# LayerNorm channel sums folded on GpSimd, and three convolution taps a slot in the last two chunks, in a Conformer and stick-breaking attention layer

## The chip, the cores and the metric

One core of a Trainium2 chip runs the whole program: TensorE (matmul), VectorE, ScalarE, GpSimd, and SyncE, which here issues every DMA. In the profile they are PE (and PEld for its weight loads), DVE, ACT, POOL and SP. The metric is the device time of one execution in microseconds (us); lower is better.

## The reference, cut to what matters

```python
h = _rmsnorm(x, g_mix)
a, gate, q, k, v = jnp.split(h @ w_in, [...], axis=-1)
u = a * jax.nn.sigmoid(gate)                                   # 512 channels
c = _causal_dwconv(u_ext, w_dw) + b_dw                         # 31 taps, each channel by itself
c = jax.nn.silu(_layernorm(c, g_cn, b_cn)) @ w_pw              # LayerNorm over the 512 channels
o = _stick_breaking(rmsnorm(q), rmsnorm(k_all), v_all, ...)    # 8 heads x 64
x = x + jnp.concatenate([c, o], axis=-1) @ w_out
f = jax.nn.relu(_rmsnorm(x, g_ff) @ w_ff1)
x = x + (f * f) @ w_ff2                                        # 4096 hidden
```

It is computed for a prompt of 2048 frames and for 64 further frames of a running stream (the sample), in fp32. `_layernorm` takes the mean over the channels, subtracts it, squares, takes the mean of the squares and scales. Weight matmuls are made of three passes over values split in a high and a low part.

## The kernel before, in words

The prompt is cut into four chunks of 512 frames (0 to 3); the 64 sample frames ride with chunk 3. Channels lie on the 128 partitions, so the convolution's sum of a chunk is four blocks (k = 0 to 3) of 128x512, held in `cacc` (in `cacc_second` for chunk 1). In chunk 3 a tap covers 606 columns, and the LayerNorm runs once over 512 columns and once over the sample's 64.

The order of all work is written out by hand in slots. A slot is one step of TensorE's main work, and every engine walks the same list of slots, each in its own program order. Chunk c+1's tail of convolution, LayerNorm, pointwise projection (`pw`) and attention is woven into the slots of the feed-forward of chunk c (`window(c)`: eight rounds e of 16 slots, of which the first eight are `f1` slots, 12 matmuls each, and the last eight are `f2` slots, 12 matmuls each). For chunk 0 the tail is woven into `front()`: 92 slots of six matmuls that compute the projections of chunk 1. `window(2)`, `window(1)` and `window(0)` thus hold the tails of chunks 3, 2 and 1.

Within a slot an engine takes its parts in a fixed order. VectorE first splits new weights if due (`w_s<-w_raw`), then runs `convolve(late_taps)`, then the step of `ln`, then `pw`, then its add of a finished `f2` result (`resid<-ps`) or, in every second `f1` slot, the low part of the hidden values (`hid_lo`), which waits for three passes of ScalarE over the matmul result. TensorE does the step of `ln`, then `pw`, then the slot's main matmuls, then the steps of attention.

The last `LATE[c]` taps of a chunk (20, 43, 36, 28 of 124) run in the slots before `ln0(c)`, two a slot. Then LN_STEPS steps follow, one a slot: 0 TensorE multiplies each of the four blocks with a 128x128 matrix of ones (`ones`, true fp32), which adds up the channels over blocks and partitions into PSUM; 1 VectorE takes off the mean (L1803), ScalarE squares into `csq` (L1402); 2 TensorE does the same four matmuls over `csq`; 3 and 4 the reciprocal root; then the scaling, the sigmoid, GpSimd's `cid` (L1162) and the split into `cT_hi` and `cT_lo`. The sample's piece follows eight slots behind. `pw_slot(c)` is the slot after the last step, `att_first(c)` is five slots later (nine for chunk 0), and attention fills the slots to `att_past(c)` (58 for chunk 0, 116 otherwise) evenly.

| chunk | ln0 before / after | pw_slot before / after | att_first before / after |
|---|---|---|---|
| 0 | 10 / 10 | 22 / 24 | 31 / 33 |
| 1 | 22 / 22 | 34 / 36 | 39 / 41 |
| 2 | 18 / 12 | 30 / 26 | 35 / 31 |
| 3 | 14 / 10 | 34 / 32 | 39 / 37 |

Weights pass through a ring of eight slabs of 1 MB (`w_s`, RING = 8). `weight_order()` puts the two `pw` slabs behind the four `f1` slabs of round `e == pw_slot(c + 1) // 16`. The load of slab n may go out when slab n - 8 is free (L774), and an `f2` slab is free when all the `f2` slots of its round are done. SyncE issues in program order, so what stands behind a DMA that waits, waits too.

## Time and profile before

| | |
|---|---|
| median of 3 runs | 2778.92 us (2776.28 to 2780.08) |
| span of the profiled execution, from its first to its last instruction | 2777.2 us |
| mean granted TensorE clock of the core | 0.990 |
| PE busy, DVE busy, ACT busy, POOL busy | 97%, 60%, 39%, 16% |
| HBM traffic over the span | 221 GB/s |

The span is 1.7 us under the median of the runs. A matmul of 128x512 in a run of them takes 0.39 us from its start to its end in the rows, but the next starts 0.23 us after it: they overlap, and it is the distance between starts that counts. A true fp32 matmul stands in the rows as two MATMUL records. "PEclk" is the granted clock as a share of 2.4 GHz; 0.5 is 1.2 GHz. The time in square brackets is how long the engine was idle before the row, and who ended that.

### The profile page before, as it was taken

How to read it: one execution, taken by the hardware profiler on the slowest of the kernel's cores; microseconds unless marked ns; L12 is line 12 of the kernel's file. 1: busy time of each engine (PE TensorE's matmuls, PEld its weight loads, DVE VectorE, ACT ScalarE, POOL GpSimd, SP SyncE). 2: the span in 40 equal slices, each digit the busy share in tenths (PEclk: the TensorE clock that was granted, in tenths of full speed). 3: DMA queues.
4: the chain of work that ended last, by engine and by line, in shares of the span. 5: the costliest groups of instructions: out<-in, count | busy, mean ns of one | idle time of the engine just before them, and what ended most of it. 6: DMA issues, size and time to landing. Idle time of an engine off the chain costs nothing. (4 is left out here: it accounts for less than half of the span.)

```text
span 2777.2 us, 37645 instructions
## 1 busy us (share of the span) xinstructions
PE 2687.2 (97%) x14000; PEld 2270.3 (82%) x14000; DVE 1663.9 (60%) x2621; ACT 1069.5 (39%) x2146; POOL 453.3 (16%) x462
## 2 busy tenths in 40 slices
PE   8988899999999999999999999999999999999999
PEld 6757778788887887788888797778888887998998
DVE  6996767577763576377775368627888842222122
ACT  4434524455552122355553212335666631221211
POOL 2122210022210010032221102103333310000000
PEclk9999999999999999999999999999999999999999
DMA  9795797697769568455554747845355456443532
GB/s 330 255 349 188 237 355 266 259 336 253 256 218 375 214 233 282 184 209 185 168 187 165 284 186 237 291 163 190 118 181 191 150 188 248 187 177 122 212 152 95
DMA packets 262048, 616.21 MB, mean 222 GB/s; under 512 B 23217, under 2 KB 159409, under 8 KB 213741
## 3 DMA queue, kind: packets, MB, share of 16 engines
q1 hardware_dynamic: 261869, 613.80, 61.8%
q8 instruction: 115, 1.88, 0.3%
q14 instruction: 64, 0.52, 0.1%
HBM read 444.79 MB, written 168.94 MB: 221 GB/s over the span
## 5 line engine op out<-in xcount | busy, mean ns | idle before, releaser
L2020 PE MATMUL ps<-h2T_hi,w_s 128*128 128x512 f32 (+2 forms) x1312 | 469.2, 358 | 7.9 <-DMA w_s<-w_scratch 3.9
L2022 PE MATMUL ps<-h2T_hi,w_s 128*128 128x512 f32 (+2 forms) x1312 | 458.3, 349 | 0.0
L1174 POOL TENSOR_TENSOR beta<-beta,stay 128x512 f32<-128x512 f32 (+3 forms) x328 | 313.0, 955 | 889.5 <-DVE stay L1859 853.4
L2021 PE MATMUL ps<-h2T_lo,w_s 128*128 128x512 f32 (+2 forms) x1312 | 457.9, 349 | 0.0
L1929 DVE TENSOR_TENSOR resid<-ps,resid 128x512 f32<-128x512 f32 x256 | 174.6, 687 | 261.3 <-PE ps L2285 260.6
L1451 ACT ACTIVATE stay<-ps 128x512 f32<-128x512 f32 (+3 forms) x328 | 174.8, 533 | 347.2 <-PE ps L2221 227.1
L2283 PE MATMUL ps<-w_s,hid_hi 128*128 128x512 f32 x768 | 308.3, 401 | 0.0
L2284 PE MATMUL ps<-w_s,hid_lo 128*128 128x512 f32 x768 | 299.9, 390 | 0.0
L2285 PE MATMUL ps<-w_s,hid_hi 128*128 128x512 f32 x768 | 299.8, 390 | 0.0
L1526 ACT ACTIVATE ps<-ps 128x512 f32<-128x512 f32 (+1 forms) x160 | 81.3, 508 | 542.7 <-PE ps L2022 542.7
L2020 PEld LDWEIGHTS ps<-h2T_hi,w_s 128*128 128x128 f32 x1312 | 248.0, 189 | 38.3 <-DMA w_s<-w_scratch 4.0
L1859 DVE TENSOR_TENSOR_SCAN stay<-stay,stay,ones 128x512 f32<-128x512 f32 x192 | 274.4, 1430 | 0.0
L2022 PEld LDWEIGHTS ps<-h2T_hi,w_s 128*128 128x128 f32 x1312 | 247.8, 189 | 30.9
L2021 PEld LDWEIGHTS ps<-h2T_lo,w_s 128*128 128x128 f32 x1312 | 248.2, 189 | 26.6 <-issue 1.0
L1651 DVE SCALAR_TENSOR_TENSOR cacc<-uT,vecs,cacc 128x512 f32<-128x512 f32 (+1 forms) x360 | 259.6, 777 | 1.5
L1939 DVE TENSOR_TENSOR hid_lo<-ps,hid_hi 128x512 fp32r<-128x512 f32 x96 | 66.3, 691 | 261.8 <-ACT hid_hi L1536 261.8
L1869 DVE TENSOR_TENSOR aT_lo<-ps,aT_hi 128x512 fp32r<-128x512 f32 (+3 forms) x328 | 189.6, 578 | 14.6 <-ACT aT_hi L1463 8.8
L2221 PE MATMUL ps<-a_k,a_q 128*128 128x512 f32 (+3 forms) x640 | 186.9, 371 | 8.8 <-DMA a_k<-k_scratch 6.9
L2231 PE MATMUL ps<-ident,beta 128*128 128x128 f32 (+1 forms) x1104 | 175.1, 274 | 7.4 <-DVE aT_lo L1869 7.3
L1463 ACT CAST aT_hi<-ps 128x512 fp32r<-128x512 f32 (+3 forms) x328 | 173.6, 529 | 19.3 <-PE ps L2231 14.7
L1452 ACT ACTIVATE beta<-ps 128x512 f32<-128x512 f32 (+3 forms) x328 | 173.6, 529 | 0.0
L2285 PEld LDWEIGHTS ps<-w_s,hid_hi 128*128 128x128 f32 x768 | 144.2, 188 | 31.9
(217 smaller groups left out, 5179.1 us busy)
## 6 DMA issues: line engine op xcount, KB each, us to landing
w_s<-w_scratch SPq DMA_DIRECT2D x282, 1024.0 KB, 7.5
w_scratch<-w_s SPq DMA_DIRECT2D x94, 1024.0 KB, 8.3
w_raw<-in_w_ff SPq DMA_DIRECT2D x64, 512.0 KB, 5.7
a_k<-k_scratch SPq DMA_DIRECT2D x80, 256.0 KB, 3.8
a_v<-v_scratch SPq DMA_DIRECT2D x80, 256.0 KB, 4.0
a_q<-q_scratch SPq DMA_DIRECT2D x64, 256.0 KB, 4.4
w_raw<-in_w_in SPq DMA_DIRECT2D x20, 512.0 KB, 7.7
mix_scratch<-ohl SPq DMA_DIRECT2D x66, 128.0 KB, 3.0
```

Of the source, the lines that this page charges most:

```text
L1174: nc.gpsimd.tensor_tensor(v[0:q.r, 0:n], v[0:q.r, 0:n], stay_of(q.z)[0:q.r, 1:n + 1], ALU.mult).then_inc(s_a, 1)
L1651: nc.vector.scalar_tensor_tensor(out=acc, in0=uT[:, k, tap:tap + wd], scalar=vecs[:, k, tap:tap + 1], in1=acc, op0=ALU.mult, op1=ALU.add). ...
L1859: nc.vector.tensor_tensor_scan(v[0:q.r, 0:q.n][:, ::-1], v[0:q.r, 0:q.n][:, ::-1], ones[0:q.r, 0:1].to_broadcast([q.r, q.n]), init, ALU.mu ...
L1869: ins = nc.vector.tensor_tensor(aT_lo[:, o, 0:full, q.t * P:q.t * P + q.r], bank[:, 0:full * q.r].rearrange("p (a b) -> p a b", a=full), a ...
L2020: nc.tensor.matmul(out, w[0], x[0], start=start, stop=False)
L2021: nc.tensor.matmul(out, w[0], x[1], start=False, stop=False)
L2022: return nc.tensor.matmul(out, w[1], x[0], start=False, stop=stop)
L2221: ins = nc.tensor.matmul(ps[0:q.r, Z_BANK + q.z % 2, 0:q.n], x, a_k[:, k0:k0 + q.n], start=v == 0, stop=v == 1)
L2231: ins = nc.tensor.transpose(ps[0:w, T_BANK + q.z % 2, b * q.r:(b + 1) * q.r], beta[q.z % 4][0:q.r, b * P:b * P + w], ident[0:q.r, 0:q.r])
L2283: nc.tensor.matmul(o, hid_hi[x][:, k, q0:q0 + r], wh[:, c0:c0 + BANK], start=k == 0, stop=False)
L2284: nc.tensor.matmul(o, hid_lo[x][:, k, q0:q0 + r], wh[:, c0:c0 + BANK], start=False, stop=False)
L2285: ins = nc.tensor.matmul(o, hid_hi[x][:, k, q0:q0 + r], wl[:, c0:c0 + BANK], start=False, stop=k == 3)
```

## The change

Three things. First, GpSimd adds the four blocks (two adds into `csq`, then one more) before the mean, and the four squared blocks before the variance; TensorE then does one matmul with `ones` where it did four. Second, these adds have steps of their own: LN_STEPS is 14 instead of 12, and all later steps move by one or by two. Third, chunks 2 and 3 issue three late taps a slot, so `ln0` of chunk 2 goes from 18 to 12 and that of chunk 3 from 14 to 10.

```diff
-LN_STEPS = 12
+LN_STEPS = 14
+def taps_a_slot(c):
+    return 3 if c > 1 else 2
 def ln0(c):
-    return (LATE[c] + 1) // 2
+    return -(-LATE[c] // taps_a_slot(c))
...
         def late_taps(c, slot):
-            return range(min(TAPS, TAPS - LATE[c] + 2 * slot), min(TAPS, TAPS - LATE[c] + 2 * slot + 2))
+            n = taps_a_slot(c)
+            return range(min(TAPS, TAPS - LATE[c] + n * slot), min(TAPS, TAPS - LATE[c] + n * (slot + 1)))
...
 # GpSimd
             def ln(c, n, step):
                 a, q0, w = conv_pieces(c)[n]
                 lb = c + n
-                k = step - 5
+                if step == 0:
+                    if c == 1:
+                        pool.wait_ge(out_ps, 8)
+                    pool.wait_ge(kvq_ps, 12 * c + 3 * len(tiles(c)))
+                    if n:
+                        pool.wait_ge(yn_ok, CB * lb)
+                    for h in range(2):
+                        for k in (2 * h, 2 * h + 1):
+                            pool.wait_ge(taps, TAPS * c + taps_in_order[c].index((k, CW - 1)) + 1)
+                        nc.gpsimd.tensor_tensor(csq[:, h, 0:w], conv_sum(c, 2 * h, a, w), conv_sum(c, 2 * h + 1, a, w),
+                                                ALU.add).then_inc(folded, 1)
+                    pool.wait_ge(folded, 6 * lb + 2)
+                    nc.gpsimd.tensor_tensor(csq[:, 0, 0:w], csq[:, 0, 0:w], csq[:, 1, 0:w], ALU.add).then_inc(folded, 1)
+                if step == 3:
+                    for h in range(2):
+                        pool.wait_ge(sq_ok, CB * lb + 2 * h + 2)
+                        nc.gpsimd.tensor_tensor(csq[:, 2 * h, 0:w], csq[:, 2 * h, 0:w], csq[:, 2 * h + 1, 0:w],
+                                                ALU.add).then_inc(folded, 1)
+                    pool.wait_ge(folded, 6 * lb + 5)
+                    nc.gpsimd.tensor_tensor(csq[:, 0, 0:w], csq[:, 0, 0:w], csq[:, 2, 0:w], ALU.add).then_inc(folded, 1)
+                k = step - 7
...
 # ScalarE: squares at step 2 (was 1), Ln and Exp at 5 (was 3), sigmoids from 7 (was 5), high parts from 9 (was 7)
 # VectorE: mean taken off at step 2 (was 1), lnv at 5 (was 3), scaling from 6 (was 4), products from 8, low parts from 10
 # TensorE
             def ln(c, n, step):
                 a, q0, w = conv_pieces(c)[n]
                 lb = c + n
-                if step == 0:
+                if step == 1:
                     if n:
                         pe.wait_ge(xc_ok, CB * lb)
-                    for k in range(CB):
-                        pe.wait_ge(taps, TAPS * c + taps_in_order[c].index((k, CW - 1)) + 1)
-                        ins = nc.tensor.matmul(ps[:, Z_BANK, 0:w], ones[:], conv_sum(c, k, a, w), start=k == 0, stop=k == CB - 1)
-                    ins.then_inc(mean_ps, 1)
-                if step == 2:
+                    pe.wait_ge(folded, 6 * lb + 3)
+                    nc.tensor.matmul(ps[:, Z_BANK, 0:w], ones[:], csq[:, 0, 0:w], start=True, stop=True).then_inc(mean_ps, 1)
+                if step == 4:
                     if n:
                         pe.wait_ge(var_ok, lb)
-                    for k in range(CB):
-                        pe.wait_ge(sq_ok, CB * lb + k + 1)
-                        ins = nc.tensor.matmul(ps[:, Z_BANK + 1, 0:w], ones[:], csq[:, k, 0:w], start=k == 0, stop=k == CB - 1)
-                    ins.then_inc(var_ps, 1)
+                    pe.wait_ge(folded, 6 * lb + 6)
+                    nc.tensor.matmul(ps[:, Z_BANK + 1, 0:w], ones[:], csq[:, 0, 0:w], start=True, stop=True).then_inc(var_ps, 1)
```

Three places show how the instructions move. The first is VectorE in `window(0)`, at the LayerNorm of chunk 1 (slots 21 to 25), before: `hid_lo` is the low part of the hidden values, `w_s<-w_raw` the split of a new weight slab, and the rows that wait for `mean_ps` take off the mean.

```order
L1651 SCALAR_TENSOR_TENSOR cacc_second_72<-uT,vecs,cacc_second_72 128x512 [waits taps]
L1939 TENSOR_TENSOR hid_lo_103<-ps,hid_hi_102 128x512 [waits f_hi]
L1611 TENSOR_TENSOR w_s<-w_raw,w_s 128x1024 [waits hi_done]
L1803 SCALAR_TENSOR_TENSOR cacc_second_69<-ps,cacc_second_69 128x512 [waits mean_ps]
L1803 SCALAR_TENSOR_TENSOR cacc_second_70<-ps,cacc_second_70 128x512
```

The same place in the changed kernel:

```order
L1675 SCALAR_TENSOR_TENSOR cacc_second_72<-uT,vecs,cacc_second_72 128x512 [waits taps]
L1963 TENSOR_TENSOR hid_lo_103<-ps,hid_hi_102 128x512 [waits f_hi]
L1635 TENSOR_TENSOR w_s<-w_raw,w_s 128x1024 [waits hi_done]
L1963 TENSOR_TENSOR hid_lo_103<-ps,hid_hi_102 128x512 [waits f_hi]
L1635 TENSOR_TENSOR w_s<-w_raw,w_s 128x1024 [waits hi_done]
L1827 SCALAR_TENSOR_TENSOR cacc_second_69<-ps,cacc_second_69 128x512 [waits mean_ps]
L1827 SCALAR_TENSOR_TENSOR cacc_second_70<-ps,cacc_second_70 128x512
```

The subtraction of the mean now stands behind a second `hid_lo` (that of slot 23) and a second weight split. The second place is TensorE in `window(2)`, at the first `pw` of chunk 3, which waits for its slab (`w_in2`), before:

```order
L2021 MATMUL ps<-h2T_lo_84,w_s 128x512
L2022 MATMUL ps<-h2T_hi_83,w_s 128x512
L2020 MATMUL ps<-cT_hi,w_s 128x512 [waits w_in2,c_lo]
L2021 MATMUL ps<-cT_lo,w_s 128x512
L2022 MATMUL ps<-cT_hi,w_s 128x512
```

And in the changed kernel:

```order
L2304 MATMUL ps<-w_s,hid_lo_103 128x512
L2305 MATMUL ps<-w_s,hid_hi_102 128x512
L2044 MATMUL ps<-cT_hi,w_s 128x512 [waits w_in2,c_lo]
L2045 MATMUL ps<-cT_lo,w_s 128x512
L2046 MATMUL ps<-cT_hi,w_s 128x512
```

Before, the 24 matmuls of two `f1` slots (`h2T`) stood between the last `f2` matmul of round 1 (`hid_hi`) and this `pw`; now it follows that matmul at once. The third place is SyncE in `front()`, where attention of chunk 0 begins: `a_q` and `a_k` are loads of queries and keys, `w_s` of weight slabs. Before:

```order
L895 DMA a_q<-q_scratch 128x2x256 [waits z_ps]
L774 DMA w_s<-w_scratch 128x2048 [waits w_st2,pw_ps]
L774 DMA w_s<-w_scratch 128x2048 [waits w_st3,pw_ps]
L774 DMA w_s<-w_scratch 128x2048 [waits ag_ps] x2
L886 DMA a_k<-k_scratch 128x512 [waits z_ps]
```

And in the changed kernel:

```order
L901 DMA a_q<-q_scratch 128x2x256 [waits z_ps]
L780 DMA w_s<-w_scratch 128x2048 [waits w_st3,pw_ps]
L780 DMA w_s<-w_scratch 128x2048 [waits w_st4,pw_ps]
L780 DMA w_s<-w_scratch 128x2048 [waits ag_ps]
L892 DMA a_k<-k_scratch 128x512 [waits z_ps]
```

Three slabs instead of four are issued between the first query load and the next keys.

## Rows read from the trace of the kernel before

**Rows 1.** The page, part 1: busy time and share of each engine.
```profile
PE 2687.2 (97%) x14000; PEld 2270.3 (82%) x14000; DVE 1663.9 (60%) x2621; ACT 1069.5 (39%) x2146; POOL 453.3 (16%) x462
```
**Rows 2.** Timeline of PE, chunk 0's LayerNorm: start us, us, instruction, [idle before, releaser].
```profile
172.18 1.88 PE L2178 MATMUL ps<-cacc,ones 128*128 128x512 f32 x4
...
177.56 1.19 PE L2178 MATMUL ps<-cacc,ones 128*128 128x512 f32 x2 [1.90 <-DVE cacc L1651]
...
182.86 3.59 PE L2185 MATMUL ps<-csq,ones 128*128 128x512 f32 x8
...
186.52 0.39 PE L2021 MATMUL ps<-hT_second_lo,w_s 128*128 128x512 f32 x1
```
**Rows 3.** Timeline of PE, the sample's two sums in chunk 3.
```profile
1809.27 1.00 PE L2178 MATMUL ps<-cacc,ones 128*128 128x64 f32 x8
```
**Rows 4.** Timeline of PE, DVE and ACT at chunk 1's LayerNorm.
```profile
487.88 2.84 PE L2178 MATMUL ps<-cacc_second,ones 128*128 128x512 f32 x6 [1.59 <-DVE cacc_second L1651]
...
487.07 2.07 DVE L1651 SCALAR_TENSOR_TENSOR cacc_second<-uT,vecs,cacc_second 128x512 f32<-128x512 f32 x3
...
490.80 2.48 DVE L1803 SCALAR_TENSOR_TENSOR cacc_second<-ps,cacc_second 128x512 f32<-128x512 f32 x4
498.09 0.69 DVE L1939 TENSOR_TENSOR hid_lo<-ps,hid_hi 128x512 fp32r<-128x512 f32 x1 [4.81 <-ACT hid_hi L1536]
498.69 1.21 DVE L1611 TENSOR_TENSOR w_s<-w_raw,w_s 128x1024 fp32r<-128x1024 f32 x1
...
491.51 2.42 ACT L1402 ACTIVATE csq<-cacc_second 128x512 f32<-128x512 f32 x4 [3.29 <-DVE cacc_second L1803]
496.24 0.58 ACT L1526 ACTIVATE ps<-ps 128x512 f32<-128x512 f32 x1 [2.30 <-PE ps L2022]
```
**Rows 5.** The line of GpSimd's multiply of two tiles: duration ns min/median/max.
```profile
L1174 POOL TENSOR_TENSOR beta<-beta,stay x328: 408/1092/2011, 229.4 to 2259.1; 128x512 f32<-128x512 f32 x96, 128x127 f32<-128x127 f32 x32, 128x383 f32<-128x383 f32 x32, 64x191 f32<-64x191 f32 x4
```
**Rows 6.** Timeline of DVE, chunk 2's taps in window(1).
```profile
1072.72 2.73 DVE L1651 SCALAR_TENSOR_TENSOR cacc<-uT,vecs,cacc 128x512 f32<-128x512 f32 x4
...
1078.43 0.69 DVE L1929 TENSOR_TENSOR resid<-ps,resid 128x512 f32<-128x512 f32 x1 [0.46 <-PE ps L2285]
```
**Rows 7.** Timeline of DVE and ACT, chunk 3's taps in window(2).
```profile
1747.03 3.12 DVE L1651 SCALAR_TENSOR_TENSOR cacc<-uT,vecs,cacc 128x606 f32<-128x606 f32 x4
...
1763.49 0.58 ACT L1526 ACTIVATE ps<-ps 128x512 f32<-128x512 f32 x1 [3.63 <-PE ps L2022]
```
**Rows 8.** Timeline of PE, four waits elsewhere.
```profile
246.94 0.45 PE L2221 MATMUL ps<-a_k,a_q 128*128 128x128 f32 x1 [6.07 <-DMA a_k<-k_scratch]
...
1169.45 0.79 PE L2020 MATMUL ps<-h2T_hi,w_s 128*128 128x512 f32 x1 [3.88 <-DMA w_s<-w_scratch]
...
1845.89 0.47 PE L2020 MATMUL ps<-cT_hi,w_s 128*128 128x512 f32 x1 [0.56 <-DMA w_s<-w_scratch]
1861.65 0.80 PE L2020 MATMUL ps<-cT_hi,w_s 128*128 128x512 f32 x1 [3.23 <-DVE pwo L1839]
```
**Rows 9.** Windows: us, busy us (x) of PE, PEld, DVE, ACT, POOL; PEclk, DMA share, GB/s.
```profile
240.00:270.00 30.00, 22.92 (x125) 19.95 (x123) 21.29 (x37) 14.78 (x40) 8.15 (x11) 0.83 0.57 175
270.00:300.00 30.00, 25.57 (x161) 21.77 (x160) 28.65 (x51) 21.00 (x58) 14.99 (x15) 1.00 0.67 193
...
1150.00:1180.00 30.00, 25.61 (x102) 20.48 (x101) 4.29 (x8) 7.33 (x16) 1.05 (x2) 0.89 0.66 260
...
1780.00:1880.00 100.00, 95.92 (x436) 76.72 (x434) 30.47 (x65) 36.55 (x67) 5.83 (x8) 0.98 0.50 187
```
**Rows 10.** Timeline of SP (issues) and, last, of PE where round 2's first matmul starts.
```profile
230.86 2.46 SPq L774 DMA_DIRECT2D w_s<-w_scratch  x4
233.36 0.74 SPq L886 DMA_DIRECT2D a_k<-k_scratch  x1
...
1838.36 0.39 PE L2020 MATMUL ps<-h2T_hi,w_s 128*128 128x512 f32 x1
```
**Rows 11.** The line of the slab loads, 1838 to 1850: from issue to landing.
```profile
DMA to landing us min/median/max: 4.7/8.9/10.9
```

More of the change, by code:

```diff
@@ L492, in build @@
         vp_out = [sem(f"vp_out{i}") for i in range(2)]
-        lg_ok, sd_ok, id_ok, nwt = sem("lg_ok"), sem("sd_ok"), sem("id_ok"), sem("nwt")
-        mean_ps, xc_ok, sq_ok, var_ps, var_ok, lnr_ok, yn_ok, sg_ok, cm_ok, c_hi, c_lo, cvo_ps, cvo_ok, cvo_out = (
-            sem(n) for n in ("mean_ps", "xc_ok", "sq_ok", "var_ps", "var_ok", "lnr_ok", "yn_ok", "sg_ok", "cm_ok",
+        lg_ok, sd_ok, id_ok = sem("lg_ok"), sem("sd_ok"), sem("id_ok")
+        folded, mean_ps, xc_ok, sq_ok, var_ps, var_ok, lnr_ok, yn_ok, sg_ok, cm_ok, c_hi, c_lo, cvo_ps, cvo_ok, cvo_out = (
+            sem(n) for n in ("folded", "mean_ps", "xc_ok", "sq_ok", "var_ps", "var_ok", "lnr_ok", "yn_ok", "sg_ok", "cm_ok",
                              "c_hi", "c_lo", "cvo_ps", "cvo_ok", "cvo_out"))
@@ L1396, in ln @@
                 nt = len(tiles(c))
-                if step == 1:
-                    if n:
-                        act.wait_ge(yn_ok, CB * lb)
+                if step == 2:
                     for k in range(CB):
@@ L1402, in ln @@
                         nc.scalar.activation(csq[:, k, 0:w], conv_sum(c, k, a, w), ACT.Square).then_inc(sq_ok, 1)
-                if step == 3:
+                if step == 5:
                     act.wait_ge(var_ok, lb + 1)
@@ L1408, in ln @@
                     nc.scalar.activation(unused[:], ident[:, 0:1], ACT.Sigmoid)
-                k = step - 5
+                k = step - 7
                 if 0 <= k < CB:
@@ L1415, in ln @@
                                          bias=vecs[:, k, CW + 2:CW + 3], scale=vecs[:, k, CW + 1:CW + 2]).then_inc(sg_ok, 1)
-                if step == 7 and n == 0:
+                if step == 9 and n == 0:
                     for m in (2 * nt - 2, 2 * nt - 1):
@@ L1422, in ln @@
                     act.wait_ge(vo_out[1], 16 * (2 * c + 2))
-                k = step - 7
+                k = step - 9
                 if 0 <= k < CB:
@@ L1799, in ln @@
                 lb = c + n
-                if step == 1:
+                if step == 2:
                     dve.wait_ge(mean_ps, lb + 1)
@@ L1804, in ln @@
                                                        in1=conv_sum(c, k, a, w), op0=ALU.mult, op1=ALU.add).then_inc(xc_ok, 1)
-                if step == 3:
+                if step == 5:
                     dve.wait_ge(var_ps, lb + 1)
                     nc.vector.tensor_scalar(lnv[:, 0:w], ps[:, Z_BANK + 1, 0:w], 1.0 / CC, EPS, ALU.mult, ALU.add).then_inc(var_ok, 1)
-                if step == 4:
+                if step == 6:
                     dve.wait_ge(sd_ok, lb + 1)
                     nc.vector.scalar_tensor_tensor(out=ntmp[:, 0:w], in0=lnr[:, 0:w], scalar=-0.5, in1=lnr[:, 0:w],
-                                                   op0=ALU.mult, op1=ALU.mult).then_inc(nwt, 1)
-                    dve.wait_ge(nwt, 2 * lb + 1)
-                    nc.vector.tensor_tensor(ntmp[:, 0:w], ntmp[:, 0:w], lnv[:, 0:w], ALU.mult).then_inc(nwt, 1)
-                    dve.wait_ge(nwt, 2 * lb + 2)
+                                                   op0=ALU.mult, op1=ALU.mult).then_inc(lnr_ok, 1)
+                    dve.wait_ge(lnr_ok, 3 * lb + 1)
+                    nc.vector.tensor_tensor(ntmp[:, 0:w], ntmp[:, 0:w], lnv[:, 0:w], ALU.mult).then_inc(lnr_ok, 1)
+                    dve.wait_ge(lnr_ok, 3 * lb + 2)
                     nc.vector.scalar_tensor_tensor(out=lnr[:, 0:w], in0=ntmp[:, 0:w], scalar=1.5, in1=lnr[:, 0:w],
                                                    op0=ALU.add, op1=ALU.mult).then_inc(lnr_ok, 1)
-                    dve.wait_ge(lnr_ok, lb + 1)
+                    dve.wait_ge(lnr_ok, 3 * lb + 3)
                     dve.wait_ge(xc_ok, CB * (lb + 1))
-                for k in {4: (0,), 5: (1, 2), 6: (3,)}.get(step, ()):
+                for k in {6: (0,), 7: (1, 2), 8: (3,)}.get(step, ()):
                     nc.vector.tensor_tensor(conv_sum(c, k, a, w), conv_sum(c, k, a, w), lnr[:, 0:w],
                                             ALU.mult).then_inc(yn_ok, 1)
-                k = step - 6
+                k = step - 8
                 if 0 <= k < CB:
@@ L1827, in ln @@
                                             ALU.mult).then_inc(cm_ok, 1)
-                k = step - 8
+                k = step - 10
                 if 0 <= k < CB:
```

## The prediction

> **What bounds the kernel now.** I read the page first: PE is busy for 97% of the span and no other engine for more than 60% [rows 1]. So the time is TensorE's list of slots, and only three things change it: the length of its work, its waits, and stretches at a lower clock. Next came the groups of instructions and the timeline of PE at the LayerNorms, for the price of the matmuls that go; then DVE and ACT at the same places, because TensorE will now wait for a chain through them and GpSimd; then the list of PE's waits over the whole span, because nearly every step of the three tails moves by two to six slots, and waits that hang on a slot number move too.
>
> The price of a matmul with `ones`: four of them start at 182.86, and the second ordinary matmul behind them starts at 186.52 [rows 2]. Less the 0.23 of one ordinary matmul that is 3.43 us, 0.86 each. For the sample's 64 columns eight records take 1.00 us, so 0.25 for each of four [rows 3].
>
> **Part 1: matmuls removed.** Each full piece loses six of eight: 4 pieces x 6 x 0.86 = 20.6 us. The sample loses 6 x 0.25 = 1.5. Together -22.1 us, all of it on the path.
>
> **Part 2: the waits for the folds.** A fold of 128x512 isn't in the trace; the nearest row is GpSimd's multiply of two tiles, 1.09 us in the median, 2.01 at most [rows 5]. I take 1.1 us, since it is the same instruction with another operation. The bounds are 0.8 (three quarters of the median) and 2.0. Only two folds lie behind the last tap: that of blocks 2 and 3 and the final one, 2.2 us. Before the variance it is again two, behind the last square. TensorE covers the first with one slot of work (step 0), the second with what is left of three.
>
> Chunk 0, where a slot is six matmuls, 1.37 us. The last tap ends at 177.5 (TensorE's last fourth waits for it until 177.56), while TensorE is at slot 10 at 172.18 and its next ordinary matmul starts at 178.12 [rows 2]: 5.9 us for 3.4 of work, so 2.4 us of waits. Now slot 11 begins at 173.55 and the mean can start at 177.5 + 2.2 + 0.2 for semaphores = 179.9: a wait of 6.3 us, +3.9. Mean taken off and squares need some 3.3 us after it, the folds 2.2: that is 186.4, and TensorE is then at about 187, so no second wait.
>
> Chunk 1, slots of 12 matmuls, 2.72 us. The last three taps run 487.07 to 489.1, and TensorE waits 1.59 us to 487.88 [rows 4]. TensorE comes to slot 23 at 485.26 + 2.72 = 488.0, the folds end at 491.4: wait 3.5 instead of 1.6, +1.9. The variance is worse. The order of instructions shows the subtraction of the mean behind the `hid_lo` of slot 23 and a weight split. Slot 23 ends at 495.0; three ScalarE passes (496.24 to the 498.09 of the next row) are 1.85, `hid_lo` 0.6, the split 1.2, the four subtractions 2.5, the last square 0.7 behind them [rows 4], the folds 2.2: 504.1. TensorE is at slot 26 at 500.5. +3.6 us.
>
> Chunk 2: four taps take 2.73 with overlap, 0.66 each [rows 6]. From 1072.72 the six taps of slots 8 and 9, two adds, three taps, an add and three taps end at 1082.5; slot 10's result comes at 1078.4, so slot 13 begins at 1083.9 and the folds end at 1084.8: +0.9. The variance comes out +0.5 by the same count (subtraction behind slot 13's add). Chunk 3: a tap of 606 columns takes 0.76, and from 1747.03 DVE has four times six taps and a `hid_lo`, and four more taps: 1770.75. TensorE begins slot 8 at 1763.4 [rows 7], slot 11 at 1771.6, the folds end at 1773.0: +1.4, +0.3 for a `hid_lo` that is late at slot 9, +0.5 at the variance. The sample's mean in slot 19 now waits for the scaling of the main piece at slot 18 and three short folds: +1.7 (0 to 3.4).
>
> Sum of waits: 3.9 + 1.9 + 3.6 + 1.4 + 2.2 + 1.7 = +14.7 us.
>
> **Part 3: the clock.** After a wait of 3.23 us ending at 1861.65 the granted clock over 1780 to 1880 is 0.98, and after 3.88 us it is 0.89 over 30 us, after 6.07 us 0.83 over 30 us [rows 8, 9]: 1.7 to 2 us, 3.3 and 5.1 us lost, some of it within the wait. For chunk 1's two waits of 3.5 us I take 1.7 each, for chunk 0 0.9 more than now (it has such a stretch already). +4.3. The lower bound is 0, if no clock falls.
>
> **Part 4: slabs and keys.** Chunk 3's `pw` moves from slot 34 to slot 32, the first of round 2, and its slab may be loaded only when the `f2` slots of round 1 are done: at that very moment (second place of the order). TensorE was there at 1838.36 [rows 10]; the first of the loads lands 4.7 us after its issue [rows 11], at 1843.3; the second slab was waited for until 1845.89 at slot 34, by 0.56 us [rows 8]. Now the first `pw` waits 5.0 us and, 1.4 us of matmuls later, again until 7.5 us after the slot's start: 6.2 of waits, against 0.6. With a clock stretch between those of 3.88 and 6.07 us this is +5.6 + 2.6 = **+8.2 us**. Nothing covers it: `pw` stands ahead of the slot's own matmuls.
>
> Chunk 2's wait of 3.88 us at 1169.45 goes. It is for slab `f1` of round 2, third quarter, which takes the place of `pw`'s first slab: free in slot 34, needed in slot 36, with SyncE held by the `pw` stores. Now it is free at slot 30. With its clock (3.3 us less 0.4 within the wait) -6.8. A wait of 0.6 for `pw`'s slab in chunk 1 goes as well (slot 34 to 36).
>
> In `front()` the keys of the third head are issued at 233.36 behind four slabs, and TensorE waits 6.07 us for them [rows 8, 10]. Now three slabs stand ahead. Between 233 and 246.9 some 4 MB moved, so a slab is worth about 3 us: -2.9, the clock unchanged.
>
> Sum: +8.2 - 6.8 - 0.6 - 2.9 = -2.1.
>
> **Part 5: attention.** Chunk 0's 41 steps now fill 25 slots, not 27. In 270 to 300 DVE is busy for 28.65 of 30 us [rows 9], so packing more steps there costs up to two slots of TensorE's work, 2.7 us, and nothing if TensorE is the later; I take +1.3. Chunks 2 and 3 get four and two slots more, chunk 1 two fewer; PE isn't idle there by more than tenths, 0.
>
> **The sum:** -22.1 + 14.7 + 4.3 - 2.1 + 1.3 = **-3.9 us**: a span of 2773.3 us, and with the 1.7 us that the median lies above the span 2775.0.
>
> **Where the skill and the rows differ.** The median of 1.09 us was measured while DVE scanned beside it, and the longest of that line is 2.01 [rows 5]. The Trainium skill, GPSIMD Engine Reference, "Specifications", says that GpSimd shares its SBUF interfaces with VectorE, with contention when a VectorE instruction has two SBUF inputs. The taps are such instructions; by that rule the folds would run nearer to the 2.0 us, and the rival below on slow folds is what it would make of the time. "Engine selection" on the same page says to add on VectorE, as GpSimd is some 2x slower; 0.69 us on DVE against 1.09 here agrees in direction.
>
> **The rivals.** About 0.2%, 5.6 us, is what this measurement can tell from no change.
>
> Forecast, 44%: the gain of the matmuls is nearly eaten, result within 0.2%, 2773.4 to 2784.
>
> First rival, 38%, faster by more than 0.2%: the waits are half of what I count, because VectorE's lag at the end of the taps shrinks once TensorE is the one that is later, or the clock doesn't fall after 3.5 us. Half of 19.0 is 9.5: 2765.5. For it: the wait of 1.59 us was followed by no slower matmuls. Against it: chunk 1's chain is counted from rows with no slack in it. If all waits vanished the time would be 2756; I give that 3% of these 38.
>
> Second rival, 10%, slower: the folds take 2.0 us. Two folds behind the last tap and two behind the last square in four pieces are 16 folds x 0.9 = +14.4: 2789.4. It decides from a fold of about 1.7 us on. It would also lengthen the taps beside them. Against it: GpSimd stands still otherwise in these slots, and after the last tap DVE has little to do.
>
> Third rival, 8%, slower: `front()` is bound by DVE and not by TensorE. Chunk 0's terms above are -5.2 for matmuls, +3.9 and +0.9 for the wait and its clock, -2.9 for the keys, +1.3 for attention: -2.0. If DVE sets the pace, matmuls and keys give nothing back, DVE stands still while GpSimd folds (+3.9), and the two slots of attention cost their full 2.7: +6.6, which makes 2783.6, and beyond 2784.5 with a fold of 1.3 us or more. It decides if DVE has no idle time between slots 31 and 58. For it: 28.65 of 30 us. Against it: DVE is idle for 8.7 us of the 30 us before [rows 9].
>
> **The range.** Folds at 0.8 us give -5 (16 x 0.3) and no clock falls -4.3: 2765.7. Folds of 1.5, the sample's wait at 3.4, a slab wait with 1 us more and the full squeeze give +6.4 + 1.7 + 1 + 1.4: 2785.5. So 2765 to 2786, which leaves out 2 in 10. Faster 0.38, same 0.44, slower 0.18.
>
> **What the profile after would show.** PE's matmuls with `ones` down to a fourth. Waits of PE for GpSimd's fold: about 6.3 us in chunk 0, 3.5 twice in chunk 1, about 1 us at means and 0.5 at variances in chunks 2 and 3. A wait of 5 us for `w_s` at the first matmul on `cT_hi` of chunk 3, and none of 3.88 us after chunk 2's `pw`. A fold's mean near 1.1 us. The prediction is wrong if waits for folds are absent or above 20 us in sum, if the wait at chunk 3's `pw` isn't there, or if new waits stand in attention.

## The result: 0.5% slower

The changed kernel takes 2790.02 us in the median of four runs (2788.87 to 2790.59), the kernel before 2777.72 (four runs, 2776.28 to 2780.08; the three known at the forecast had 2778.92): ratio 1.005, 95% interval 1.0037 to 1.0062. The forecast was 2775.0 with a range of 2765 to 2786, so it was wrong, in sign and in range. The profiled execution spans 2787.9 us against 2777.2. Of all executions in this document one is left out of every ratio and isn't read: the profiled one of the run e8, which took 6602.86 us instead of some 2776.

The page of the changed kernel, part 1, beside [rows 1]: TensorE is busy for 12 us less, GpSimd for 34 us more, and the span is longer. (The matmuls removed are worth 22 us; the others take longer wherever the granted clock is lower, and of that there is more than before, as shown below.)
```profile
PE 2675.1 (96%) x13940; PEld 2262.2 (81%) x13940; DVE 1672.9 (60%) x2621; ACT 1066.2 (38%) x2146; POOL 487.0 (17%) x492
```
The list of PE's waits after (line waited at, releaser: us in total, times, longest). L2201 is the matmul for the mean, L2206 that for the variance, L2251 the transpose in attention.
```profile
PE ps L2251 <- DVE aT_lo L1893: 16.9, 29, 1.9
PE ps L2201 <- POOL csq L1175: 15.6, 5, 5.7
PE ps L2206 <- POOL csq L1182: 9.8, 5, 5.0
...
PE ps L2044 <- DMA w_s<-w_scratch: 5.0, 1, 5.0
```
The new waits for GpSimd are 25.4 us, not 18.7 (the values forecast for each place, added up). In the kernel before, the wait for `aT_lo` was 7.3 us in 17 pieces; nothing was forecast there. The timeline of PE after, at the new matmuls of chunks 0 to 3 and of the sample (`128x64`), at the keys of chunk 0's attention, and at chunk 3's pointwise convolution, where [rows 8] had 0.56 and 3.23:
```profile
178.37 2.08 PE L2201 MATMUL ps<-csq,ones 128*128 128x512 f32 x2 [4.59 <-POOL csq L1175]
187.25 1.13 PE L2206 MATMUL ps<-csq,ones 128*128 128x512 f32 x2 [1.59 <-POOL csq L1182]
...
249.94 0.30 PE L2241 MATMUL ps<-a_k,a_q 128*128 128x128 f32 x1 [3.09 <-DMA a_k<-k_scratch]
...
490.41 2.08 PE L2201 MATMUL ps<-csq,ones 128*128 128x512 f32 x2 [5.67 <-POOL csq L1175]
506.06 1.22 PE L2206 MATMUL ps<-csq,ones 128*128 128x512 f32 x1 [4.97 <-POOL csq L1182]
...
1085.10 1.12 PE L2201 MATMUL ps<-csq,ones 128*128 128x512 f32 x2 [1.96 <-POOL csq L1175]
1095.59 0.70 PE L2206 MATMUL ps<-csq,ones 128*128 128x512 f32 x1 [1.18 <-POOL csq L1182]
...
1767.03 1.12 PE L2201 MATMUL ps<-csq,ones 128*128 128x512 f32 x2 [1.81 <-POOL csq L1175]
1777.54 1.13 PE L2206 MATMUL ps<-csq,ones 128*128 128x512 f32 x2 [1.18 <-POOL csq L1182]
1794.80 0.41 PE L2201 MATMUL ps<-csq,ones 128*128 128x64 f32 x2 [1.59 <-POOL csq L1175]
1804.36 0.41 PE L2206 MATMUL ps<-csq,ones 128*128 128x64 f32 x2 [0.91 <-POOL csq L1182]
...
1837.05 0.77 PE L2044 MATMUL ps<-cT_hi,w_s 128*128 128x512 f32 x1 [5.00 <-DMA w_s<-w_scratch]
1856.24 0.80 PE L2044 MATMUL ps<-cT_hi,w_s 128*128 128x512 f32 x1 [3.23 <-DVE pwo L1863]
```
Why chunk 1's waits are longer than counted shows in the timelines of POOL and DVE after, there. A fold is one of GpSimd's additions. The last one behind the taps and the last one behind the squares take 2.12 us each, and each begins while VectorE splits a weight slab (L1635). The two folds behind the last tap take 3.5 us (486.89 to 490.35), and so do the two behind the last square (to 506.01), where the forecast had 2.2.
```profile
486.89 1.26 POOL L1172 TENSOR_TENSOR csq<-cacc_second,cacc_second 128x512 f32<-128x512 f32 x1 [0.69 <-DVE cacc_second L1675]
488.23 2.12 POOL L1175 TENSOR_TENSOR csq<-csq 128x512 f32<-128x512 f32 x1
501.30 2.51 POOL L1179 TENSOR_TENSOR csq<-csq 128x512 f32<-128x512 f32 x2 [10.95 <-ACT csq L1426]
503.89 2.12 POOL L1182 TENSOR_TENSOR csq<-csq 128x512 f32<-128x512 f32 x1
...
487.27 1.96 DVE L1635 TENSOR_TENSOR w_s<-w_raw,w_s 128x1024 fp32r<-128x1024 f32 x1
...
501.67 1.27 DVE L1953 TENSOR_TENSOR resid<-ps,resid 128x512 f32<-128x512 f32 x2
503.38 1.51 DVE L1635 TENSOR_TENSOR w_s<-w_raw,w_s 128x1024 fp32r<-128x1024 f32 x1 [0.44 <-ACT w_s L1258]
```
**Where the time went.** The start of work that is the same in both kernels shows it. `out(c)` is the output projection of chunk c, between two windows. The first addition to `resid` in `out(0)` comes 1.8 us sooner than before, that in `out(1)` 0.9 later (the third and all behind it 0.7 sooner), that in `out(2)` 9.6 sooner (here the 3.88 us of [rows 8] are gone), and that in `out(3)` 10.7 later. So all of the loss arises between `out(2)` and `out(3)`, nearly all of it in window(2), which holds chunk 3's LayerNorm, pointwise convolution and attention. The end of it can be measured alone: from the first addition of round 1's second products (slot 25) to that of round 7's (slot 121) lie, in every kernel, the pointwise convolution, all of chunk 3's attention and six rounds of feed-forward. I call this **the stretch**: 467.7 us before, 484.9 after. It is read from the one profiled execution of each kernel. Two windows of it in the changed kernel (columns as in [rows 9]), then the same two before:
```profile
1815.00:1875.00 60.00, 51.77 (x231) 42.60 (x230) 10.28 (x25) 7.68 (x19) 0.80 (x2) 0.89 0.33 122
1875.00:2300.00 425.00, 411.75 (x2286) 344.84 (x2285) 316.78 (x517) 236.72 (x519) 134.69 (x136) 1.00 0.50 166
```
```profile
1822.00:1882.00 60.00, 55.58 (x260) 45.75 (x260) 12.73 (x34) 11.68 (x27) 1.59 (x4) 0.97 0.42 158
1882.00:2289.00 407.00, 401.06 (x2252) 339.27 (x2251) 313.31 (x512) 237.53 (x514) 134.00 (x136) 1.00 0.50 168
```
In the first window the clock is 0.89 instead of 0.97: 60 x 0.08 = 4.8 us. In the second it is 1.00 in both, and still the work that began sooner ends later.

### The profile page after: what moved, and what is told of

Same layout as the page of the kernel before. It is cut to its first block and busy times, and to the rows that moved or that the text cites. A ratio compares the mean times of both kernels' runs of the same rounds, so it can differ in the third digit from the quotient of the medians.

```text
span 2787.9 us, 37563 instructions
## 1 busy us (share of the span) xinstructions
PE 2675.1 (96%) x13940; PEld 2262.2 (81%) x13940; DVE 1672.9 (60%) x2621; ACT 1066.2 (38%) x2146; POOL 487.0 (17%) x492
## 5 line engine op out<-in xcount | busy, mean ns | idle before, releaser
L2251 PE MATMUL ps<-ident,beta 128*128 128x128 f32 (+1 forms) x1104 | 175.8, 274 | 17.3 <-DVE aT_lo L1893 16.9
L2251 PEld LDWEIGHTS ps<-ident,beta 128*128 128x128 f32 (+1 forms) x1104 | 132.7, 140 | 56.0 <-issue 28.9
```

Source lines behind the costliest of these rows:

```text
L2251: ins = nc.tensor.transpose(ps[0:w, T_BANK + q.z % 2, b * q.r:(b + 1) * q.r], beta[q.z % 4][0:q.r, b * P:b * P + w], ident[0:q.r, 0:q.r])
```

## The experiments

Every run is compared with runs of the kernel before on the same chip. To tell the clock from the rest, each kernel's mean span over its runs is split: **lost clock** is the span times one minus its mean granted clock, **rest** is what remains (the clocks are given to 0.001, so each of the two is good to 1 or 2 us). Both stand below as the difference from before. For the changed kernel itself only one clock of before is at hand. The mean clock of a kernel moves by several thousandths from one execution to the next, so a difference of 2 us or less between two rows says nothing.

| run | ratio, 95% interval | lost clock | rest | stretch |
|---|---|---|---|---|
| changed kernel | 1.0050 (1.0037 to 1.0062) | +6 | +5 | 484.9 |
| e1 attention from slot 39 | 1.0027 (1.0016 to 1.0038) | +9.1 | -2.2 | 471.3 |
| e2 two a slot from 37 | 1.0050 (1.0038 to 1.0062) | +9.5 | +3.8 | 480.6 |
| e3 before, 79 slots | 1.0034 (1.0022 to 1.0045) | +1.6 | +7.1 | 475.2 |
| e4 slots, no additions | 1.0014 (1.0005 to 1.0023) | -0.2 | +3.8 | 483.3 |
| e5 the same, from slot 39 | 0.9964 (0.9951 to 0.9976) | -1.2 | -7.9 | 474.8 |
| e6 additions with slack | 0.9959 (0.9947 to 0.9971) | +5.5 | -15.5 | 467.7 |
| e7 additions in 2, 3 only | 0.9992 (0.9980 to 1.0004) | +0.7 | -2.5 | 474.3 |
| e8 `pw` in slot 34 | 0.9997 (0.9988 to 1.0005) | +4.3 | -4.7 | |
| e9 before, odd pairing | 1.0048 (1.0035 to 1.0060) | +3.4 | +9.6 | 478.7 |
| e10 pairs from slot 37 | 1.0040 (1.0027 to 1.0054) | +9.5 | +1.5 | 481.1 |
| e11 slack, main pieces | 0.9913 (0.9900 to 0.9927) | -3.1 | -21.1 | 467.9 |
| e12 no additions, `pw` 34 | 0.9956 (0.9943 to 0.9968) | -0.8 | -11.7 | 467.8 |
| e13 none in chunk 0 | 0.9998 (0.9989 to 1.0006) | +2.7 | -3.2 | 474.5 |
| e14 before, slot 40 | 1.0002 (0.9993 to 1.0011) | +0.2 | +0.5 | 467.5 |

**e1: chunk 3's attention from slot 39.**
```diff
 def att_first(c):
-    return pw_slot(c) + pw_step(c) * CB + 1
+    return 39 if c == NC - 1 else pw_slot(c) + pw_step(c) * CB + 1
```


> The changed kernel, but chunk 3's attention starts in slot 39 as in the kernel before, so that it again has exactly two steps in each of 77 slots. Theory A (the loss of about 10 us lies in chunk 3's attention, which in the changed kernel starts in slot 37 and has four slots of one step only): the time falls from 2790.0 to about 2780 (2777 to 2783), and TensorE's waits for aT_lo fall from 16.9 us to about 8. Theory B (the loss lies in TensorE's waits for GpSimd's additions, 25.4 us over the whole run): unchanged, 2789 to 2791. Theory C (the loss lies at chunk 3's pointwise convolution, wait of 5.0 us for its slab and half clock after it): unchanged as well.

The stretch falls by 13.5 us to 471.3 (4.8 of them are the clock, 0.97 in its first 60 us), the wait for `aT_lo` to 10.1 us. The ratio falls only to 1.0027, which is 2785.2 us on the first chip's scale (the ratio times 2777.72), where theory A had 2777 to 2783: the lost clock stays. So B and C fall as the only cause, and A alone doesn't do either.

**e2: two steps a slot from slot 37.** `att_past(3)` is 114, the rest as changed.

> The changed kernel, chunk 3's attention from slot 37 as there, but ending two slots sooner, so that every one of its 77 slots has exactly two steps. If the rhythm is what costs (slots with one step shift the two kinds of attention pieces between the two halves of a slot), about 2780, as with a start in slot 39. If the place of the start is what costs (which of the 18 kinds of feed-forward slot each piece meets), it stays within 2 us of 2790. Theories B and C: unchanged, 2790.

Unchanged, 1.0050. By the number alone this spoke for the place of the start. The list of PE's waits in e2's stretch says otherwise: `aT_lo` is back at what it was before (5.4 us in 13 pieces), and a new wait stands beside it, at the sample's pass, which now comes two slots sooner (that this is why its queries are late is argued). e2's stretch is 9.3 us above e1's; 4.8 of that are the clock (0.89 against 0.97 in the first 60 us) and 3.3 this wait.
```profile
PE ps L2251 <- DVE aT_lo L1893: 5.2, 13, 1.0
PE ps L2241 <- DMA s_q<-q_scratch: 3.3, 1, 3.3
```
**e3: the kernel before, over 79 slots.** `att_past(3)` is 118.

> The kernel before, with chunk 3's attention spread from slot 39 over 79 slots, not 77: four slots have one step only. Nothing else differs from before. Theory A: this alone costs 8 to 11 us, 2786 to 2789, with waits for aT_lo above 12 us. Theories B and C: within 2 us of before, 2776 to 2780.

1.0034, rest +7.1 us: the spreading costs by itself, with no addition and no moved slot. Its `aT_lo` wait in the stretch is 10.0 us. The starts of the `resid` additions show where it costs. The slots with one step are 39, 58, 78 and 98. Against before, slots 41 to 57 take 2.5 us more, 73 to 89 3.4 and 89 to 105 1.8, and all of these hold broken pairs; slots 57 to 73, where the pairs are whole, take 0.5 less. Slots 105 to 121, where attention now ends two slots later, take 1.7 more.

**e4: the changed kernel's slots without the additions.**
```diff
 # GpSimd's additions are removed; TensorE's ln(), step 1 (mean), below; step 4 (variance) on csq likewise
-                    pe.wait_ge(folded, 6 * lb + 3)
-                    nc.tensor.matmul(..., ones[:], csq[:, 0, 0:w], start=True, stop=True)
+                    for k in range(CB):
+                        pe.wait_ge(taps, ...)
+                        ins = nc.tensor.matmul(..., ones[:], conv_sum(c, k, a, w), start=k == 0, stop=k == CB - 1)
```


> The changed kernel with all its slots, but with the LayerNorm's sums made on TensorE as before (four matmuls with ones each time) and no additions on GpSimd. Theory A: the additions and the matmuls that they save nearly cancel (22.1 us of matmuls come back, 25.4 us of waits and some 3 us of half clock go, of which 2 to 4 us of waits for the last tap and the last square come back), so 2787 to 2791, and the 10 us lost in chunk 3's attention stay. Theory B: the time falls to 2780 or less.

1.0014, on the first chip's scale 2781.6, which neither theory had. The loss in attention stays (stretch 483.3), but 10 us go elsewhere: the additions aren't neutral. The windows of chunks 0 and 1, first of the changed kernel, then of e4: PE has 16 us more busy time in e4, POOL 18 less, and the clock is 0.95 and 1.00 instead of 0.93 and 0.96.
```profile
160.00:420.00 260.00, 224.12 (x1068) 182.50 (x1068) 199.73 (x300) 108.61 (x225) 57.66 (x56) 0.93 0.82 277
420.00:560.00 140.00, 129.36 (x645) 108.63 (x645) 89.00 (x118) 57.18 (x81) 13.84 (x12) 0.96 0.69 257
```
```profile
160.00:420.00 260.00, 230.04 (x1111) 187.54 (x1110) 198.49 (x304) 109.53 (x226) 49.55 (x52) 0.95 0.83 283
420.00:560.00 140.00, 139.02 (x682) 115.14 (x682) 92.29 (x128) 59.93 (x87) 3.89 (x5) 1.00 0.75 275
```
Also, with the matmuls one slot (mean) and two slots (variance) later, e4 doesn't wait for the last tap at all: its matmuls at 175.92 and 183.48 have no idle time ahead. The slack was worth something; the additions used it up and more.

The next theory, A2, has both causes, and the next four runs test it. From here on the LayerNorm's steps are written with three small functions: `folds(c)` (additions or not), `mean_late(c)` and `var_late(c)` (slots by which TensorE's two sums and all behind them come later than in the kernel before; the changed kernel has 1 and 2).

**e5: e4 with attention from slot 39** (`folds` 0).

> The changed kernel's slots, without GpSimd's additions (TensorE sums as before), and chunk 3's attention from slot 39. Theory A2 (two causes: the clock and the waits that the additions bring, and the broken pairing of attention steps; they add up): the first is gone as in the run without additions (+3.8 us against before), the second as in the run from slot 39; 7 us less than without additions, so 2 to 5 us faster than before (ratio 0.998 to 0.9995). Rival (the two hang together: the pairing costs only what the clock does after it): the same as the run without additions, ratio 1.001 to 1.002.

0.9964, 14 us below e4's ratio and 10 faster than before, where A2 had 7 and 2 to 5. So the pairing costs without the additions too, and the rival falls. Against e1, which differs from e5 by the additions alone, it is 17 us faster.

**e6: additions with slack.**
```diff
+def mean_late(c):
+    return 2 if c else 1
+def var_late(c):
+    return 4 if c else 2
```


> The changed kernel, but in chunks 1 to 3 TensorE takes the sum for the mean one slot later still, and that for the variance two slots later, so that a slot of 2.7 us stands between each pair of additions and the matmul that needs it. Chunk 3's pointwise convolution then falls in slot 34 and its attention in slot 39. Theory A2: the additions are harmless where nobody waits for them; TensorE's waits for GpSimd fall from 25 us to below 12 (those of chunk 0 and of the sample stay), the time at half clock falls to that of before, and 12 to 20 us of matmuls are gained: ratio 0.993 to 0.996. Rival (GpSimd's additions slow VectorE and ScalarE beside them, so that the delay only moves): ratio above 0.999.

0.9959, as expected, but the clock was not: 5.5 us more lost than before. Nor were the waits for GpSimd, expected below 12 us: they are 16.3 us in four, 6.66 and 1.45 in chunk 0, 3.01 in chunk 1, 5.08 at the sample.

**e7: additions in chunks 2 and 3 alone** (`folds` and `mean_late` 1, `var_late` 2 there, 0 elsewhere; attention from slot 39).

> Chunks 0 and 1 as in the kernel before (four matmuls with ones, their slots); chunks 2 and 3 as in the changed kernel, chunk 3's attention from slot 39. Theory A2: the expensive waits (4.6, 1.6, 5.7 and 5.0 us) were those of chunks 0 and 1 and brought the half clock; without them the lost clock is that of before (about 26 us) and the rest is 2 to 5 us less, ratio 0.998 to 1.0. Rival (every wait for an addition costs clock, short ones too): ratio above 1.001.

0.9992 and +0.7 us of clock: as expected. Its six waits for additions, of 0.91 to 1.96 us, cost little clock.

**e8: the pointwise convolution in slot 34** (`pw_slot(3)` is `ln0 + LN_STEPS + 10`, which puts attention at 39).

> The changed kernel with chunk 3's pointwise convolution two slots later (slot 34, as before) and its attention from slot 39; the additions stay. Against the run with attention from slot 39 alone this takes away only the wait of 5.0 us for the convolution's slab. Theory A2: about 5 us less and 0 to 2 us of clock less than there, which was 1.0027 of before: ratio 1.0003 to 1.001. Rival (the slab is waited for later, in a slot that then comes sooner): unchanged, 1.0027.

0.9997: 8 us below e1, of which 2.5 are rest and 4.8 clock. Its trace isn't read (see the result), so that the wait for the slab went isn't shown.

**e9: the kernel before, with every pair broken.**
```diff
 # att_past
-    return 58 if c == 0 else 116
+    return 58 if c == 0 else 117 if c == NC - 1 else 116
 # att_steps
+    if c == NC - 1:
+        return range(min(n, max(0, 2 * (slot - a) - 1)), min(n, max(0, 2 * (slot - a) + 1)))
```


> The kernel before, but in chunk 3's attention the first slot (39) has one step and every later one two, the last one again (78 slots). So each pair of attention pieces that belong together (the two query tiles of one unit, the second of which multiplies by the values) falls on two slots instead of one, in all of the window. Theory P (what costs is the pairing: with an odd number of steps done, the units straddle the slots; the changed kernel had that in half of its slots): 10 to 18 us more than before, ratio 1.004 to 1.0065. Rival Q (a slot with one step costs by itself, some 2 us each): 2 slots instead of 4, ratio 1.0005 to 1.0015.

1.0048: theory P holds, Q falls. The trace shows a steady loss: the `resid` additions of each round of 16 slots come 2.5 to 3.2 us later than those of the round ahead of it, against before. One such round in PE's timeline, first before, then in e9:
```profile
2026.79 0.63 PE L2231 MATMUL ps<-ident,beta 128*128 128x128 f32 x4 [0.59 <-DVE aT_lo L1869]
...
2038.41 0.52 PE L2231 MATMUL ps<-ident,beta 128*128 128x128 f32 x3 [0.52 <-DVE aT_lo L1869]
...
2049.66 0.63 PE L2231 MATMUL ps<-ident,beta 128*128 128x128 f32 x4 [0.16 <-DVE aT_lo L1869]
```
```profile
2027.66 0.52 PE L2233 MATMUL ps<-ident,beta 128*128 128x128 f32 x3 [1.13 <-DVE aT_lo L1871]
...
2032.99 0.63 PE L2233 MATMUL ps<-ident,beta 128*128 128x128 f32 x4 [0.26 <-DVE aT_lo L1871]
...
2039.26 0.63 PE L2233 MATMUL ps<-ident,beta 128*128 128x128 f32 x4 [0.56 <-DVE aT_lo L1871]
...
2051.30 0.63 PE L2233 MATMUL ps<-ident,beta 128*128 128x128 f32 x4 [0.94 <-DVE aT_lo L1871]
...
2063.02 0.63 PE L2233 MATMUL ps<-ident,beta 128*128 128x128 f32 x4 [0.50 <-DVE aT_lo L1871]
```
These are all of the round's waits for `aT_lo`: 3.4 us instead of 1.3. The remaining 0.8 us or so of each round has no recorded wait.

**e10: the changed kernel with its steps in pairs.**
```diff
+    if c == NC - 1:
+        return range(n // 2 * (slot - a) // (b - a) * 2, n // 2 * (slot - a + 1) // (b - a) * 2)
```


> The changed kernel with one rule added: chunk 3's attention takes its 154 steps in 77 pairs over slots 37 to 115, so that a slot has two steps or none. Theory P: as with a start in slot 39, ratio 1.002 to 1.003, against 1.005 for the changed kernel, and none of the 3.3 us wait for the sample's queries that came when attention ended two slots sooner. Rival Q: as the changed kernel, 1.004 to 1.006.

1.0040 is Q's number, and its interval takes in both, so the ratio decides nothing and the verdict has to come from the profile. The rest is +1.5 against +5 in the changed kernel, and the wait for `aT_lo` in the stretch 5.1 us instead of 11.9: the pairing is mended. The stretch is still 481.1, 13.4 above before. Of that 6.8 are slab and clock: e5, e7 and e13, with the same slab wait and the same clock of 0.89 in their first 60 us, have 474.3 to 474.8. Another 1.7 are a second fall of the clock to half (1.2 GHz), for 3.4 us from 1895 on, and 1.9 a new wait for GpSimd's product. About 3 us remain open.
```profile
PE ps L2253 <- DVE aT_lo L1895: 5.1, 14, 0.6
PE ps L2253 <- POOL beta L1202: 1.9, 1, 1.9
```
**e11: slack, and additions on the main pieces of chunks 1 to 3 alone** (e6 with `folds(0)` 0, and the sample's two sums by matmul).

> The run with slack before TensorE's sums, and without the additions in chunk 0 and on the sample's piece, where it still waited 6.7 and 5.1 us for GpSimd: there TensorE sums as before. Chunks 1 to 3 keep the additions on their main pieces. Theory A2: 12 us of waits go, 6.7 us of matmuls come back, and 2 to 4 us of half clock go: 8 to 11 us less than with slack alone (0.9959), ratio 0.992 to 0.993. Rival (the waits move to VectorE's last taps, since TensorE gets there sooner): ratio 0.995 or more.

0.9913, 23 us faster than before: better than the expected 0.992 to 0.993. One wait for GpSimd is left:
```profile
PE ps L2218 <- POOL csq L1188: 3.0, 1, 3.0
```
**e12: e5 with the pointwise convolution in slot 34.**

> No additions on GpSimd at all, the changed kernel's slots, but chunk 3's pointwise convolution in slot 34 and its attention from slot 39. Against the run without additions and attention from slot 39 (0.9964) only the wait of 4.9 us for the slab goes, and the half clock behind it: 5 to 8 us less, ratio 0.9935 to 0.9945. If this is not more than 3 us above the run with slack on the main pieces, the additions on GpSimd are worth nothing even where nobody waits for them; theory A2 says that they are worth 10 to 14 us (16 matmuls of 0.86 us less the waits left), so that this run is some 3 to 8 us slower than that one.

0.9956, not the 0.9935 to 0.9945 that was expected: the stretch falls from 474.8 to 467.8, which is before's, but the whole kernel gains only 2 us on e5. Up to `out(2)` the two are the same program, yet e12's profiled execution comes to the stretch 5.2 us later: its granted clock over the first 420 us is 0.95, e5's 0.97. It stands 12 us above e11, where 3 to 8 were expected: additions on three main pieces, with one wait of 3.0 us left, are worth some 12 us. (e11 also has its sums one and two slots later in chunks 1 to 3, and attention of chunks 1 and 2 two slots later; that this part is worth nothing wasn't tested.)

**e13: no additions in chunk 0** (`folds(0)` 0, attention from slot 39).

> The changed kernel with chunk 3's attention from slot 39, and without the additions in chunk 0, where TensorE sums as before. Reference: the same with chunk 0's additions, ratio 1.0027, 35 us lost to the clock (span times one minus the mean granted clock). If chunk 0's wait is what costs the clock: 27 to 30 us lost, ratio 1.0 or below. If chunk 1's two waits cost it: 33 us or more lost, ratio 1.002 or more. Waits and matmuls of chunk 0 themselves nearly cancel (6.2 us of waits against 5.2 us of matmuls and 2.4 us of waits for the last tap).

0.9998, with 29.8 us lost to the clock instead of 35.3: chunk 0's additions cost 5.5 us of clock, or 6.4 when each run is held against the kernel before on its own chip, more than the 4.3 us that the forecast had for chunks 0 and 1 together. Against e7, which lacks chunk 1's additions and their slots too, 2 us more are lost, no more than the clocks can tell.

**e14: the kernel before, with attention from slot 40.** `att_past(3)` is 117.

> The kernel before with chunk 3's attention in slots 40 to 116 instead of 39 to 115, two steps in each. If the odd or even place matters (the results of the first feed-forward product come in every second slot): 2 to 6 us slower, ratio 1.001 to 1.002, and in the trace a constant loss in each round of 16 slots. If only pairs that straddle slots cost: within 1 us of before in the profiled spans, ratio 0.9995 to 1.0005.

1.0002, stretch 467.5: whether attention starts in an odd or an even slot doesn't matter here. That theory falls, and the last 3 us of e10 stay open.

## Why the prediction was wrong

**Where the miss lies.** The forecast's terms add up to -2.0 us for chunk 0, +3.1 for chunk 1, -10.6 for chunk 2 and +5.4 for chunk 3. From start to start of the `out` parts the trace has -1.8, +2.7, -10.5 and +20.3. So the first three chunks came out within a few tenths, or within 2 us if later additions of `out(1)` are taken, and the miss of 15 us lies in chunk 3. Of it 10.3 are the step named next, 1.6 the waits for folds there (5.5 instead of 3.9), and 1.7 a stretch at 1.2 GHz in `out(2)` (granted clock 0.50 from 1565.0 to 1568.4), which the kernel before doesn't have there; the rest isn't accounted for. That the first two sums agree is in part luck. In chunk 0 a wait of 4.56 us for queries (`a_q`, at 308.40) is new and one of 5.80 us for ScalarE (at 311.44 before) is gone, neither of them forecast; and chunk 1's waits are 3.5 us longer than counted, made up for by something that no run singles out.

**The step that failed is Part 5**: "Chunks 2 and 3 get four and two slots more, chunk 1 two fewer; PE isn't idle there by more than tenths, 0." It asked whether there is idle time to lose, not what the two slots do to the order. Before, 154 steps in 77 slots are two in each. VectorE does a slot's first step ahead of the feed-forward result and the second behind it. The two query tiles of a unit, the second of which releases the values' matmuls, stood in one slot. In 79 slots four have one step (37, 56, 76 and 96), and from the first to the second and from the third to the fourth each unit straddles two slots. e3 puts it at +7.1 us of rest in the kernel before, e9 with all slots so at +9.6 (its stretch +11.0), e4 against e5 at 11.7, the changed kernel against e1 at 7; and the changed kernel's stretch is 10.3 above that of e13, which has the same slab wait and the same clock of 0.89 in its first 60 us. So where the forecast had 0, the runs have 7 to 12 us, 10.3 of them in the changed kernel's own trace; 6.5 of these stand in its list of waits (11.9 us for `aT_lo` in the stretch, 5.4 before). That VectorE's order within the slot is the mechanism was argued from the code; that the pairing is the cause was shown. "New waits stand in attention" was on the list of what would make the forecast wrong.

**Waits for the folds, +14.7.** Chunk 0 was forecast as one wait of 6.3 and was 4.59 + 1.59, 6.2, which is luck: the folds behind the last tap began at 175.65 and not at 177.5, so the first wait was shorter, and the second, for which none was forecast, came from folds that took 1.60 to 1.75 us beside VectorE's taps. Chunk 1 was 5.67 and 4.97, not 3.5 and 3.6; chunk 2 1.96 and 1.18, not 0.9 and 0.5; chunk 3's main piece 1.81 and 1.18, not 1.7 and 0.5; the sample 2.5, not 1.7. In sum 6.7 us too little. The fold was 1.26 to 1.29 us in the median where I took 1.1, and 2.12 twice beside a slab split. The second rival, folds of 2.0 us throughout, was not the case; its time of 2789.4 is close to 2790.0 for other reasons.

**The clock, +4.3, and +4.0 with the terms of Part 4.** The profiled executions lose 36 us after against 28 before, the changed kernel's runs 6 us more than before, and the other runs with the additions where the changed kernel has them (e1, e2, e10) 9.1 to 9.5 us more. e13 puts about 6 of it on chunk 0, where I had 0.9, with the reason that a half-clock stretch stood there already; chunk 1's two waits, priced at 3.4, cost some 2 by e13 against e7, if anything.

**Matmuls, -22.1.** The price holds where hardly anybody waits: e11 against e12 gives 12 us for 15.5 of matmuls on three pieces (18 x 0.86) less a wait of 3.0.

**Slabs and keys, -2.1.** The wait at chunk 3's slot 32 was 5.00 us, as forecast; the wait of 3.88 in chunk 2 went, and `out(2)` starts 9.6 us sooner. The keys' wait fell from 6.07 to 3.09, near the 2.9 of the forecast. For the slab with its clock the forecast had 8.2: e8 against e1 gives 8 us, the stretches of e5 and e12 give 7.0, but their whole times only 2, with intervals that leave room for 7.

**Chunk 0's attention, +1.3, and the third rival.** `out(0)` comes sooner, not later, so VectorE doesn't set the pace there as the third rival had it.

Without the failed step the forecast is still off: e1, which has whole pairs and all else as in the changed kernel, is 7.5 us slower than before, where the sum said 3.9 faster. That would be 2785.2, just inside the range; it is the broken pairs that put the time outside it.

## What to carry to other kernels

When slots are added to or taken from a loop that is filled by a division such as `n * (slot - a) // (b - a)`, write down how many steps each slot gets before and after: an exact two a slot is a property of the schedule, and losing it cost more than any single wait of this change. Work taken off the bounding engine is a gain only if what replaces it has slack ahead of its reader: here all the additions without slack cost 10 us (the changed kernel against e4) or 17 (e1 against e5), while those on three main pieces, with one or two slots more, gained 12 (e11 against e12). And price a wait on TensorE with its clock: here 25 us of waits came with 6 to 9 us of lost clock.

## What the runs showed of the hardware

**GpSimd and VectorE hold each other up.** A 128x512 addition of two SBUF tiles on GpSimd took 1.26 to 1.29 us in the median, and 2.12 when it began during VectorE's 128x1024 split (above). The other way round, 20 convolution taps take 13.71 us before, 0.69 each, and beside GpSimd's additions one takes 1.63 and four take 5.64, as DVE's timeline of the changed kernel in chunk 0 shows; the additions run from 177.00 to 178.32 and from 182.52 to 187.20.
```profile
177.24 1.63 DVE L1675 SCALAR_TENSOR_TENSOR cacc_second<-uT,vecs,cacc_second 128x512 f32<-128x512 f32 x1
...
182.89 5.64 DVE L1675 SCALAR_TENSOR_TENSOR cacc_second<-uT,vecs,cacc_second 128x512 f32<-128x512 f32 x4
```
The Trainium skill, GPSIMD Engine Reference, "Specifications", says that the two share their SBUF interfaces, with contention when a VectorE instruction has two SBUF inputs. The splits and the taps have, and the rows agree, in both directions. They show more: in each of these rows the instruction that began second ended about one usual duration after the first one's end (the tap of 177.24 ends 0.55 us after the fold beside it, the folds of 488.23 and 503.89 end 1.12 us after the splits), as if it had waited. And `resid<-ps`, one of whose inputs is in PSUM, holds nothing up: two take 1.27 us from 501.67 on, beside two folds in 2.51.

**The same waits don't always cost clock.** With waits of 5.00 and 3.23 us the changed kernel's granted clock is 0.89 over the 60 us of the window above, 6.6 us lost; e1 has waits of 5.03 and 3.23 there and 0.97, 1.8 us lost; e5, e7 and e13 have 0.89. Over the first 420 us, where e12 and e5 are the same program, the granted clock was 0.95 in the one's execution and 0.97 in the other's. So one profile doesn't size the clock's term, and e1's runs lie between 2777.1 and 2786.8 us. What decides it wasn't tried.
